# Two norms, a broadcast of statistics by transposes, and the mean taken off by another engine

## What is computed

```python
def layer_norm(x):
    mu = jnp.mean(x, -1, keepdims=True)
    var = jnp.mean(jnp.square(x - mu), -1, keepdims=True)
    return (x - mu) * lax.rsqrt(var + EPS)

def modulate(x, shift, scale):  return layer_norm(x) * (1 + scale) + shift
def post_norm(x, y, gate, g, b): return layer_norm(ALPHA * x + gate * y) * g + b

x = post_norm(x, mix_lat, g1, ln1_g, ln1_b)                 # "p1", followed by
ffn = conv_ffn(modulate(x, sh2, sc2), ...)                  # a second norm of its result
x = post_norm(x, ffn, g2, ln2_g, ln2_b)                     # "p2", followed by
proj = rms_norm(x, g_mix) @ w_in                            # an RMS norm of its result
```

## Time and profile before

| | |
|---|---|
| median of 3 runs | 2066.24 us (2064.33, 2066.24 and one far off at 3383.63) |
| span of the profiled execution | 2063.5 us (it is known by its span alone) |
| PE busy | 2019.7 us, 98% |
| PEld busy | 1583.8 us, 77% |
| DVE busy | 1133.2 us, 55% |
| ACT busy | 867.1 us, 42% |
| POOL busy | 919.6 us, 45% |
| HBM traffic | 93 GB/s over the span |

### The profile page before, as it was taken

How to read it: one execution, slowest core, us unless ns; L and a number is a source line. 1 busy time by engine, 2 the same in 40 slices (tenths; PEclk the granted TensorE clock), 3 DMA queues, 4 the chain that set the end, 5 groups by cost and what they waited for, 6 DMA issues and landing times.

```text
span 2063.5 us, 26379 instructions
## 1 busy us (share of the span) xinstructions
PE 2019.7 (98%) x10212; PEld 1583.8 (77%) x10212; DVE 1133.2 (55%) x2017; ACT 867.1 (42%) x1381; POOL 919.6 (45%) x1160
## 2 busy tenths in 40 slices
PE   6999999999999999999999999999999999999998
PEld 3877677888888768768888888786776888888877
DVE  5366758997393579955522231466896543222235
ACT  4542434443232556784322222445578432222242
POOL 1344205876566325541555555302355155555540
PEclk9999999999999999999999999999999999999999
DMA  9134641222323211103333323322111333332331
GB/s 327 41 110 140 202 132 50 94 96 81 118 82 102 88 41 42 62 22 119 96 102 102 94 91 102 100 71 82 42 42 42 102 94 101 102 102 82 102 102 62
DMA packets 188299, 194.26 MB, mean 94 GB/s; under 512 B 8592, under 2 KB 184080, under 8 KB 187792
## 3 DMA queue, kind: packets, MB, share of 16 engines
q1 hardware_dynamic: 187600, 189.44, 28.3%
q10 hardware_dynamic: 576, 3.15, 0.4%
HBM read 190.48 MB, written 2.10 MB: 93 GB/s over the span
## 4 chain that ended last, share of the span: by engine, by line
PE 90%; DVE 5%; ACT 2%; POOL 2%; DMA 1%; issue 1%; SPq 0%; DVEq 0%; ACTq 0%; POOLq 0%
PE ps L808 20%; PE ps L810 20%; PE ps L809 20%; PE ps L827 3%; PE ps L829 3%; PE ps L828 3%; PE ps L855 2%; PE ps L844 1%; DVE mix L2475 1%; PE ps L846 1%; PE ps L845 1%; POOL wl L2858 1%; PE ps L1353 1%; PE ps L1426 1%; PE ps L1409 1%; PE ps L1372 1%
## 5 line engine op out<-in xcount | busy, mean ns | idle before, releaser
L2858 POOL TENSOR_TENSOR wl<-ring,wh 128x256 fp32r<-128x256 f32 x1008 | 754.0, 782 | 809.5 <-ACT wh L1463 809.5
L1463 ACT ACTIVATE wh<-ring 128x1024 fp32r<-128x1024 f32 (+1 forms) x298 | 308.9, 1044 | 310.4 <-PE ps L810 257.3
L808 PE MATMUL ps<-xh,wh 128*128 128x512 f32 (+1 forms) x976 | 384.0, 393 | 2.3 <-POOL wl L2858 2.3
L809 PE MATMUL ps<-xl,wh 128*128 128x512 f32 (+1 forms) x976 | 381.1, 390 | 0.0
L810 PE MATMUL ps<-xh,wl 128*128 128x512 f32 (+1 forms) x976 | 381.0, 390 | 0.0
L808 PE MATMUL ps<-acts,wh 128*128 128x512 f32 x880 | 343.5, 390 | 0.7 <-POOL wl L2858 0.4
L810 PE MATMUL ps<-acts,wl 128*128 128x512 f32 x880 | 342.4, 389 | 0.0
L809 PE MATMUL ps<-acts,wh 128*128 128x512 f32 x880 | 342.4, 389 | 0.0
L2475 DVE SCALAR_TENSOR_TENSOR mix<-ps,par,mix 128x441 f32<-128x441 f32 (+2 forms) x352 | 213.9, 696 | 32.3 <-ACT mix L1700 32.2
L808 PEld LDWEIGHTS ps<-xh,wh 128*128 128x128 f32 (+1 forms) x976 | 183.4, 188 | 47.1 <-issue 8.8
L810 PEld LDWEIGHTS ps<-xh,wl 128*128 128x128 f32 (+1 forms) x976 | 183.4, 188 | 39.3
(11 more groups left out here) (441 smaller groups left out, 3044.4 us busy)
## 6 DMA issues: line engine op xcount, KB each, us to landing
ring<-in_w_ff_dram SPq DMA_DIRECT2D x64, 1024.0 KB, 5.2
ring<-in_w_in_dram SPq DMA_DIRECT2D x28, 1024.0 KB, 5.0
ring<-in_ffn_w_up_dram SPq DMA_DIRECT2D x22, 1024.0 KB, 5.0
ring<-in_w_ada_dram SPq DMA_DIRECT2D x17, 1024.0 KB, 5.1
ring<-in_w_out_dram SPq DMA_DIRECT2D x12, 1024.0 KB, 5.2
ring<-in_ffn_w_down_dram SPq DMA_DIRECT2D x8, 1024.0 KB, 5.1
ring<-in_w_ple_gate_dram SPq DMA_DIRECT2D x8, 1024.0 KB, 5.0
early<-in_w_ada_dram SPq DMA_DIRECT2D x7, 1024.0 KB, 10.8
```

What stands on the lines that cost most here:

```text
L808: t.matmul(b[0:m, 0:n], s.hi[:, k, a:a + m], x2[0][:, k, :], start=k == ks[0], stop=False)
L809: t.matmul(b[0:m, 0:n], s.hi[:, k, a:a + m], x2[1][:, k, :], start=False, stop=False)
L1463: a.activation(s.hi[:, :, c], s.ap[:, :, c], ACT.Copy).then_inc(*up("hi", "hi", name, hf))
L2858: i = p.tensor_tensor(s.lo[:, k:k + 2, c], s.ap[:, k:k + 2, c], s.hi[:, k:k + 2, c].bitcast(F32), ALU.subtract)
```

## The change

Six edits:

1. `spread` uses `t.transpose` of the broadcast column in place of `t.matmul`, for all its callers: 16 instructions behind p1, 8 behind p2, 20 in each layer.
2. The idle products go from 4 to 3 behind p1, and from 7 to 3 behind p2.
3. DVE subtracts `dl` for slab 0 (p1) or slabs 0 and 1 (p2) itself, reading the bank (`less_mean`). POOL subtracts it from the other seven or six.
4. ACT copies `dl` out only after DVE's first subtraction has ended (the two may not read the bank together). In p1 it takes the second root before that copy.
5. In p2 the second variance moves from before the feed to behind `xl` of slab 3, and its root and reciprocal to behind slab 5 (ACT) and behind `xl` of slab 6 (DVE).
6. In p1 the bank of `dl` is freed by ACT's copy as before; in p2 by DVE's subtraction of slab 1, which waits for ACT's copy.

```diff
-                    i = t.matmul(b[:, c * 128:c * 128 + 128], src[:, c:c + 1].to_broadcast([128, 128]), ident)
+                    i = t.transpose(b[:, c * 128:c * 128 + 128], src[:, c:c + 1].to_broadcast([128, 128]), ident)
...
-                    spin(ps(first[0]), 4)
+                    spin(ps(first[0]), 3)
...
-                        spin(ps(first[0]), 7)
+                        spin(ps(first[0]), 3)
...
-                rows_of(("dl", tag), rsf)
+            def mean_rows(tag):
+                e.wait_ge(*done(("dl", tag)))
+                e.wait_ge(*at("less", tag, 0))
+                if tag == "p1":
+                    out_of(("dl", tag), rsf)
+                else:
+                    a.activation(rsf, ps(("dl", tag))[:, :], ACT.Copy).then_inc(*up("act", "dlrow", tag))
+
+            def second_root(tag):
                 e.wait_ge(*at("var2", tag))
...
             statistics("p1")
+            second_root("p1")
+            mean_rows("p1")
...
             statistics("p2")
+            mean_rows("p2")
...
                 feed("g0", j, at("hn", "p2", j), ("g_mix_2", 0), sqf, xh, done(("uv", 2, 5)), mine=False)
+                if j == 5:
+                    second_root("p2")
...
+            def less_mean(tag, j, last):
+
+                if last:
+                    e.wait_ge(*at("dlrow", tag))
+                e.wait_ge(*done(("dl", tag)))
+                i = v.tensor_tensor(mix[:, j, :], mix[:, j, :], ps(("dl", tag))[:, :], ALU.subtract)
+                i.then_inc(*(free(("dl", tag)) if last else up("vec", "less", tag, j)))
+                e.wait_ge(*(taken(("dl", tag)) if last else now("vec")))
...
             statistics("p1", True)
+            second_variance("p1", True)
+            less_mean("p1", 0, False)
+            second_inverse("p1")
...
-            e.wait_ge(*done(("R1", "p2")))
             for j in range(10):
                 if j < 8:
-                    e.wait_ge(*at("centered", "p2", j))
+                    if j < 2:
+                        less_mean("p2", j, j == 1)
+                    else:
+                        e.wait_ge(*at("centered", "p2", j))
+                    e.wait_ge(*done(("R1", "p2")))
...
                     feed("g0", j - 2, ("g_mix_2", 0), xh, xl)
+                if j == 5:
+                    second_variance("p2", False)
+                if j == 8:
+                    second_inverse("p2")
...
             def centered(tag):
-                e.wait_ge(*taken(("dl", tag)))
-                for j in range(8):
+                e.wait_ge(*(taken(("dl", "p1")) if tag == "p1" else at("dlrow", "p2")))
+                for j in range(1 if tag == "p1" else 2, 8):
                     p.tensor_tensor(mix[:, j, :], mix[:, j, :], rsf, ALU.subtract).then_inc(*up("pool", "centered", tag, j))
```

More of the change, by code:

```diff
@@ L2080, in statistics, with second_variance @@
                 v.reciprocal(inv1, roots[:, 0:4]).then_inc(*up("vec", "r1", tag))
+            def second_variance(tag, centered):
                 after()
@@ L2093, in statistics, with second_inverse @@
                 v.tensor_scalar(var_f, var_f, gk[:, 4:5], 0.0, ALU.add, ALU.max).then_inc(*up("vec", "var2", tag))
+            def second_inverse(tag):
                 e.wait_ge(*at("root2", tag))
                 v.reciprocal(inv2, roots[:, 4:8]).then_inc(*up("vec", "r2", tag))
+            def less_mean(tag, j, last):
[5 more added lines that the diff above has]
+                e.wait_ge(*(taken(("dl", tag)) if last else now("vec")))
             def inverse(tag, rs, n=T):
@@ L2409, in vector @@
                 if j < 8:
-                    e.wait_ge(*at("centered", "p1", j))
+                    if j:
+                        e.wait_ge(*at("centered", "p1", j))
                     i = v.scalar_tensor_tensor(h[:, j, :], mix[:, j, :], pc("ln1_g", j), ps(("R1", "p1"))[:, :], ALU.mult, ALU.mult)
```

## The result

The changed kernel has a median of 2060.45 us (2058.37 to 2063.60, 9 runs), the kernel before 2066.05 us (from 2063.43, 9 runs on the same chips). The medians are 5.6 us apart; the ratio is 0.9979, with a 95% interval of 0.9971 to 0.9987, which is 4.3 us less (2.7 to 6.0). That is within 2%. The time is close to the forecast of 2060.0 us, while the forecast gain of 6.2 us lies just outside the interval of the ratio. One of the nine launches of the kernel before took 3383.63 us, and three in the experiments (two of the kernel before, one without transposes) 3383 to 4084 us; these slow runs are in no ratio.

What follows compares the result with a forecast made beforehand. TensorE was taken as the bound in the layers, VectorE and POOL behind the norms. Gains of 3.6 + 0.9 + 1.7 = 6.2 us, against the 2066.24 median, gave 2060.0 us; range 2056.5 to 2065.0.

Steps and rivals of the forecast that it cites:

- The layers: Spreads as transposes in both layers: 40 instructions, each 0.091 us shorter, gain 3.6 us, with bounds of 0 and 3.6.
- some 5 us: Behind `er` in the layers: time of the 24 + 24 matmuls that don't need its result, against 3 us for the heads.
- The first norm: Feed behind the first norm: VectorE subtracts slab 0 itself and the feed gains 0.9 us, or 1.4 with `xl` undisturbed.
- So does `xl` of slab 0, at 316.0: Behind the first norm: `xl` of slab 0 ends 1.4 us sooner, as the third multiplication does.
- The 0.5 us that the forecast gave back at `xl` of slab 1: First feed: `xl` of slab 1 falls wholly under POOL and slows, reducing the gain from 1.4 to 0.9 us.
- The second norm: Feed behind the second norm: TensorE starts near 698.1 and ends at 711.1 instead of 712.77, gain 1.7 us.
- until about 700.6: Behind the second norm, before the change: seven idle products keep TensorE this long, 0.5 us too long.
- the four steps of the second variance, about 0.85 us: Second feed: time these steps take on VectorE between `xl` of slabs 3 and 4.
- 1.0 if POOL is a slab late: Second norm: lower bound of the 1.7 us gain; the upper was 2.5 if the variance is hidden.
- Idle products: Behind the norms: one fewer at the first priced 0 to 0.7, taken as 0; four fewer at the second give nothing further.
- the slower rival: Transposes and gaps leave TensorE at half clock: five extra stretches of 1.5 us, 7.5 against 6.2, so 2067.5; chance 0.08.
- The plus or minus 2 us for the clock: Whole kernel: allowance for half-clock stretches, 1.5 us each on the path, that no edit orders.

## Why the prediction was right, step by step

**The layers: the mechanism right, the term too small.** "40 x 0.091 = 3.6 us" was measured as 4.6: 1.8 us for each `er` and 0.45 for each row factor. A transpose of a broadcast column costs 0.104 us and not 0.127, the figure of the row of sixteen in the earlier trace rows. The 48 matmuls behind `er`, for which the forecast wrote "some 5 us", take 0.23 us each, so 11 us; that reason was stronger than written. In the profile after, about 0.27 us came back in each layer ahead of `er`. In all profiles this interval is 145.55 to 145.81 us without the transposes (147.28 apart) and 145.78 to 146.12 with them. The two overlap and nothing here says where the difference would come from, so that stays open.

**The first norm: the price was near, the reasoning behind it was not.** Between the two profiles it gained 1.2 us, and I had written 0.9. But the step "So does `xl` of slab 0, at 316.0" failed. The three multiplications did come sooner, by 1.55 us (1.4 forecast). `xl` then took 1.72 us, not 1.35, since it began just after GpSimd's subtraction had and waited for nearly all of it. It ends 0.55 us behind the end of a subtraction whenever it starts under one. So, as long as those ends stay where they are, it gains a whole subtraction of 1.23 us or nothing. The 0.5 us that the forecast gave back at `xl` of slab 1 were not lost there: it took 0.81 us, as before. With a full clock under the spreads the old order and the new one bring the first L1166 at 10.23 and 10.27 us: the edits are worth nothing. What the changed kernel gains in its first profile it gains against a kernel whose float32 spreads ran at half clock. There VectorE waited 0.31 us for `R2`, and 0.52 us for `m2` before that, and so came under the next subtraction. Timeline of VectorE, kernel before:

```profile
312.13 0.75 DVE L2415 SCALAR_TENSOR_TENSOR mix<-h,wt,ps 128x512 f32<-128x512 f32 x1 [0.52 <-PE ps L1138]
```

I had taken that profile as the normal case. In the other profile of the changed kernel, the product behind the feed comes at 36.02 us, as with the old order and a full clock. So this term is 0 to 1.2 us by where the half clock falls. That it came out near 0.9 is luck. I should have asked for every VectorE instruction with two SBUF inputs when GpSimd's current instruction ends, instead of carrying a duration over.

**The second norm: the start right, the middle mis-sized.** `xl` of slab 0 was forecast 2.1 us sooner, and the feed began 2.2 us sooner (9.08 to 6.88). The forecast had written 2.5 for the start of the feed, because it read that the idle products kept TensorE "until about 700.6". In the trace before the first L1210 starts at 700.21, just behind `xl`: the 6.17 us of the row are not the time until the next matmul can start. Kernel by kernel, 1.7 is from the new order (9.08 to 7.40) and 0.5 from the transposes. The forecast gain at its end was 1.7, and it is 0.75. The failing term is "the four steps of the second variance, about 0.85 us": from 705.60 to 707.31 they took 1.7, of which 1.0 is a wait for GpSimd's last subtraction. GpSimd's 1.55 us a slab (9.30/6), against the 1.47 taken from the earlier trace rows, made the wait 0.5 us longer. Both are means of two durations: in either kernel a subtraction comes every 1.23 us until an `xl` has run ahead of it, and every 1.70 us in turn with them, so leaving out two slabs took away two of the short ones. By the forecast's own times the variance began near 703.0 (`xl` of slab 4 at 705.3, less that `xl`, its multiplication and 0.85) and GpSimd ended near 703.6, so the collision stood in the numbers. I had priced the small steps as if it could not touch them. The bound "1.0 if POOL is a slab late" was the near one, and the gain lies below it. The move of the variance into the feed, which the forecast took for a gain of time at the start, gave nothing in the end, as the kernel with the variance ahead of the feed shows.

**Idle products.** Nothing, as forecast, by the runs with 3 and 3 alone. With the new order 4 and 7 cost 1.2 us in the one profile there is, under a half clock, and the ratios (0.9984 against 0.9979 and 0.9975) don't tell them apart.

**The clock and the slower rival.** The rival needed five extra stretches at half clock. Leaving out the last microseconds of each profile, the changed kernel shows five in its first profile and four in its second, at places that mostly exist in other kernels too, and the kernel before four. None followed `er`, in any of the thirteen profiles, and 96 transposes brought none either. The rival is out. The plus or minus 2 us for the clock was needed: the nine runs of the changed kernel lie between 2058.37 and 2063.60. The stretches came and went in front of the changed instructions (267), in the first feed, in the second and behind the second (743). Each lasted 3.4 us, or two of them 6.8, and cost 1.2 to 1.6 us where TensorE sets the pace.

**The sum.** 3.6 + 0.9 + 1.7 = 6.2 was forecast. The intervals of the first profile give 4.6 + 1.2 + 0.75, less 0.8 lost in the three unchanged intervals between them (0.27 each), which is 5.7; from norm 1 to the end it is 5.6. Two errors of about 1 us had opposite signs, and two of the three terms left their own bounds: the layers' 4.6 (0 to 3.6) and the second norm's 0.75 (1.0 to 2.5). The mechanism of the layers, the largest term, was right; the time of 2060.0 was right partly by luck.

**What stays open.** By their trace the transposes alone should gain about 5 us, and their ratio shows 2.5 (0.6 to 4.3). The whole change shows 4.3 and 5.2 by ratio. The edits without transposes lost 1.2 and 0.4. The parts so add up to 2 to 4 us less than the whole, with intervals of about 1.8 us on each. A part of it may be that norm 2 needs both, but the intervals (0.5, 0.24 and 0.75 us) give no room for that much. The scatter of the stretches between runs (1.2 to 1.6 us each) is large enough to hide it, and I have not shown that it is the cause.

## What to carry to other kernels

Read a VectorE instruction with two SBUF inputs beside a busy GpSimd by the instant at which GpSimd's instruction ends, never by its duration in another place. Such a step started sooner gains nothing unless it gets under an earlier GpSimd instruction. A small step put into such a phase can cost a wait for the whole instruction, so place small steps where GpSimd is idle. Where TensorE is the bound, transposes spread a value over all partitions for half of what float32 matmuls cost (0.104 us against 0.218). Before an edit is judged by two profiles, cut both at the same instructions and compare the intervals that hold no edit first.

## What the hardware did that I had not expected

- A VectorE instruction on 12 elements a partition took 1.14 to 1.15 us beside a GpSimd subtraction, in six profiles of five kernels, and 0.17 us otherwise. In one kernel, that without transposes, it took 1.14 us in the first profile and 0.17 in the second, where GpSimd was done 0.6 us before. Its neighbours of 4 elements, started after GpSimd's end, took 0.16; one of 4 elements that met a subtraction took 1.12 and 1.33 instead of 0.23. The Trainium skill (SBUF — State Buffer, "SBUF: two separate sides") describes a lock that either engine holds for a whole instruction. The trace agrees: a 128x512 `xl` ends 0.55 us behind GpSimd's subtraction, and the next subtraction takes 1.74 us instead of 1.27. That it can hold up such small work for 1 us was seen only here.
- A transpose of a broadcast float32 column costs 0.09 us in a row of 4, 0.104 in one of 16 and 0.108 in one of 96. The float32 matmul that does the same costs 0.218.
- The intervals that hold no edit differ between profiles: it took 306.0 to 309.7 us from the start to norm 1, and in the pair above 1.8 us of the difference arose before the first large product. The same instructions met a half clock in one profile and none in the next, as in layer 1 at 1491 us.
- From the product behind feed 1 to norm 2 it takes 348.3 to 348.7 us with a stretch at half clock at its beginning, and 346.8 to 347.1 without: 1.6 us for 3.4 us at half.
